# Expert loop of a two-block network: passes of 32 tokens in four bands instead of 64 in two, with the output product one pass behind

## The chip, the cores and the metric

The kernel runs as one program on one core of one Trainium2 chip. The metric is the device time in microseconds (us); lower is better. Engines are called PE (matrix products; PEld is its weight loads), DVE (vector engine), ACT (scalar engine), POOL (GpSimd) and SP (the engine whose queue issues the transfers here).

## What is computed

The reference takes 256 tokens of width 1024 through two blocks. The first holds attention, a gated recurrence and a table lookup with experts of one row each; the second holds a convolution, attention and a mixture of 32 experts. Only the last part, the mixture, is touched by the change. Cut down, it is:

```
logits = hf @ w_router + b_router            # 256 tokens, 32 experts
top_v, top_e = lax.top_k(logits, 4)
gates = softmax(top_v)
for each expert e, with the tokens xi that chose it:
    hc = xi @ w1[e] + b1[e]                  # 1024 -> 2048
    g, u = hc[:, :1024], hc[:, 1024:]
    g = minimum(g, 7.0); u = clip(u, -7.0, 7.0)
    hm = (u + 1.0) * (g * sigmoid(1.702 * g))
    y[token] += gate * (hm @ w2[e] + b2[e])  # 1024 -> 1024
x = x + g2 * y, then an RMS norm
```

All arrays are float32. An expert's weights are six units of 2 MB: four of `w1` and two of `w2`. All 32 experts have tokens, so 192 units (403 MB) are read whatever the routing is. Evaluating the reference's router on its own inputs gives the tokens of each expert, in order of the experts: 22, 36, 72, 24, 52, 13, 14, 43, 36, 29, 24, 24, 22, 39, 24, 18, 28, 58, 33, 26, 21, 21, 27, 18, 55, 38, 16, 28, 48, 44, 21, 50 (1024 in all). Experts count from 0 here.

## The kernel before

The arrays of an expert are read with a loop over passes. A pass is up to `NS` = 64 tokens of one expert; an expert with more tokens has more passes. The number of passes is known only at run time (`n_pass`, `passes_to`, `last_of`, `total_i`), and every engine runs its own loop over passes `q` and reads its tables with value loads.

On PE (`one_pass`, L1272) a pass is: `hidden` twice (L1240), the products of the 64 gathered tokens `xg` with `w1`, first the gate half into bank "Zg", then the up half into "Zu"; each product has 64 columns of stationary tokens and 512 moving weight columns, and the two halves of the 128 output partitions are two bands, `half`, that hold different weight columns. ACT copies each result to `z_sb`, `turn` (L1251) transposes it back, four 128x128 pieces each. Between these, `gather` (L1045) makes the next pass's tokens as products of `h3_rows` with the selection matrix `sel`, in two lots of eight, which ACT scales and shifts into `xg` (`modulated`, L1535). Then `combine(q)` (L1260) adds the rows `yg` of the pass before into the output in banks 0 to 3, the gated selection `selg` is transposed ("S", L1287), and the output product "D" (L1294 to L1298) multiplies this pass's `hm` with `w2`.

DVE makes `sel` for the next pass, adds the bias to the two transposed results (L2339), clips, multiplies, makes `hm` (L2349), then `selg` (L2096), then scales D's result into `yg` (L2357). The helper `mm` is L823, the helper `add` L982, transposes are L1256, L1287 and L1288.

The order of transfers is written out in SP's program. There are ten places of 2 MB: two sets of four for `w1`, of even and odd experts, and one pair (places 4 and 5) for `w2`. Ahead of the loop all six units of expert 0 and the four `w1` units of expert 1 are loaded. Then, for each expert e: after "Zg" of its last pass, the first two `w1` units of e+2; after "D" of its last pass, `w2` of e+1 and the other two `w1` units of e+2 (L717 to L727). All go through one queue.

## Time and profile before

| | |
|---|---|
| median of 3 runs | 2271.8 us (2269.18 to 2272.0) |
| the profiled execution, its own time | 2270.6 us |
| span in its profile | 2268.7 us |
| PE busy | 2073.9 us (91%) |
| DVE busy | 982.8 us (43%) |
| ACT busy | 599.0 us (26%) |
| mean granted clock of TensorE | 0.969 of 2.4 GHz |
| bytes moved | 784.36 MB |

The expert loop is the stretch from 1313 us to about 2261 us of the span. Busy time of PE is that of pipelined products whose ends are modelled, so a busy PE may be waiting inside. A float32 product stands in the trace as two MATMUL and two LDWEIGHTS records, a transpose as one of each. "PEclk" is the granted clock as a share of 2.4 GHz, so 0.50 is the level of 1.2 GHz and 1.00 that of 2.4 GHz. "DMA" is the busy share of the 16 transfer engines.

### The profile page before, as it was taken

Reading aid. Unit: us, or ns where it says so; the run is one execution under the profiler, and the core shown is the slowest. Engines: PE = TensorE matmul, PEld = TensorE weight load, DVE = VectorE, ACT = ScalarE, POOL = GpSimd, SP = SyncE. Lnnn points to the kernel's source line nnn. Section 1 sums busy time; section 2 is a strip of 40 time slices with the busy share of each in tenths; the row PEclk is TensorE's granted clock in tenths of the full one; section 3 lists DMA queues with packets and bytes.
Section 4 is the critical chain, followed back from the end, with each engine's and each line's share of the span. In section 5 each row is a group of like instructions: output and inputs, shape, how many; then the busy total and the mean of one; then the engine's idle time right before and its main releaser. Section 6 shows DMA issues by size and latency. Waiting matters only on the chain.

```text
span 2268.7 us, 27663 instructions
## 1 busy us (share of the span) xinstructions
PE 2073.9 (91%) x9026; PEld 1158.3 (51%) x9027; DVE 982.8 (43%) x2266; ACT 599.0 (26%) x1223; POOL 503.5 (22%) x562
## 2 busy tenths in 40 slices
PE   8999999988787778688999999999999999999998
PEld 7867788733333333233878744444444444433443
DVE  5955555756766766754573212111111111111112
ACT  4625401311212212222234122222222222222222
POOL 0000001677777777775000000000000000000000
PEclk9999999989889999999999999999999999999999
DMA  7352396899999999999644657899999999999996
GB/s 316 117 217 98 125 379 257 331 412 410 411 409 403 408 410 410 410 393 359 240 149 149 256 217 305 374 430 430 430 429 430 430 430 430 430 429 430 430 430 281
DMA packets 111704, 784.36 MB, mean 346 GB/s; under 512 B 13056, under 2 KB 13312, under 8 KB 80160
## 3 DMA queue, kind: packets, MB, share of 16 engines
q1 hardware_dynamic: 37920, 515.18, 54.7%
q0 software_dynamic: 73728, 268.47, 29.9%
q8 instruction: 31, 0.51, 0.1%
q14 instruction: 25, 0.20, 0.0%
HBM read 782.55 MB, written 1.05 MB: 345 GB/s over the span
## 4 chain that ended last, share of the span: by engine, by line
PE 49%; DMA 28%; POOL 11%; issue 6%; DVE 4%; ACT 2%; SPq 0%; DVEq 0%; POOLq 0%; ACTq 0%
PE ps L823 39%; DMA ring<-in_w_exp 23%; PE ps L982 8%; DMA ring<-in_peer_v,arena 4%; POOL ring L781 4%; POOL ring L783 4%; POOL arena L783 2%; POOL arena L781 1%; ACT arena L1333 1%; PE ps L1256 1%; DVE ring L2006 0%; SPq L692 0%; DVE arena L1955 0%; ACT arena L1427 0%; PE ps L955 0%
## 5 line engine op out<-in xcount | busy, mean ns | idle before, releaser
L823 PE MATMUL ps<-ring,arena 128*64 128x512 f32 (+2 forms) x2312 | 526.2, 586 | 32.9 <-DMA ring<-in_w_exp 30.2
L823 PE MATMUL ps<-arena,ring 128*128 128x256 f32 (+1 forms) x2272 | 488.1, 374 | 3.8 <-DVE arena L1749 3.2
L982 PE MATMUL ps<-ring,arena 128*128 128x512 f32 x768 | 386.1, 660 | 103.3 <-ACT arena L1333 103.2
L823 PEld LDWEIGHTS ps<-arena,ring 128*128 128x128 f32 x2272 | 419.3, 190 | 65.3 <-issue 7.8
L823 PE MATMUL ps<-arena 128*128 128x64 f32 (+4 forms) x2498 | 432.1, 419 | 11.6 <-ACT arena L1317 6.1
L823 PEld LDWEIGHTS ps<-ring,arena 128*64 128x64 f32 (+1 forms) x2312 | 177.0, 141 | 356.6 <-issue 300.4
L823 PEld LDWEIGHTS ps<-arena 128*128 128x128 f32 (+2 forms) x2498 | 266.8, 172 | 170.5 <-issue 160.5
L982 PEld LDWEIGHTS ps<-ring,arena 128*128 128x128 f32 x768 | 159.1, 212 | 325.7 <-issue 192.0
L2006 DVE CUSTOM_DVE_ANT_0 ring<-ring,ps 128x1024 f32<-128x1024 f32 x192 | 232.5, 1220 | 157.8 <-DMA ring<-in_peer_v,arena 156.9
L982 PE MATMUL ps<-arena 128*128 128x512 f32 (+2 forms) x600 | 201.9, 585 | 26.5 <-ACT arena L1333 24.8
L1661 ACT COPY arena<-ps 128x512 f32<-128x512 f32 (+1 forms) x99 | 51.0, 515 | 661.6 <-PE ps L823 628.9
L2339 DVE TENSOR_TENSOR arena<-ps,arena 128x512 f32<-128x512 f32 x66 | 45.7, 692 | 391.9 <-PE ps L1256 391.9
L781 POOL DMA_INDIRECT ring<-in_peer_u,arena x192 | 185.0, 963 | 80.0 <-issue 49.2
L783 POOL DMA_INDIRECT ring<-in_peer_v,arena x192 | 182.1, 948 | 59.8 <-issue 56.4
L982 PEld LDWEIGHTS ps<-arena 128*128 128x128 f32 (+1 forms) x600 | 83.3, 193 | 117.6 <-issue 80.8
L2357 DVE TENSOR_TENSOR arena<-ps,arena 128x512 f32<-128x512 f32 x33 | 22.8, 692 | 226.9 <-PE ps L823 226.9
L1324 ACT ACTIVATE arena<-arena 128x4 f32<-128x4 f32 (+1 forms) x67 | 19.9, 297 | 372.4 <-DVE arena L2006 372.4
L1333 ACT ACTIVATE arena<-arena 128x128 f32<-128x128 f32 x256 | 82.1, 390 | 121.7 <-DVE arena L2013 121.7
L1538 ACT ACTIVATE arena<-ps,arena 128x64 f32<-128x64 f32 x272 | 87.3, 400 | 26.8 <-PE ps L823 26.8
L2006 DVE CUSTOM_DVE_ANT_0 arena<-arena,ps 128x1024 f32<-128x1024 f32 x64 | 76.9, 1220 | 36.3 <-DMA arena<-in_peer_v,arena 35.9
L769 POOL COPY arena<-arena 128x16 uint32<-128x16 uint32 x16 | 3.3, 207 | 382.5 <-POOLq L768 382.4
L783 POOL DMA_INDIRECT arena<-in_peer_v,arena x64 | 60.6, 946 | 19.5 <-issue 17.7
(344 smaller groups left out, 1268.4 us busy)
## 6 DMA issues: line engine op xcount, KB each, us to landing
ring<-in_w_exp SPq DMA_DIRECT2D x128, 2048.0 KB, 24.9
arena<-in_w_exp SPq DMA_DIRECT2D x64, 2048.0 KB, 32.4
ring<-in_w_in SPq DMA_DIRECT2D x24, 2048.0 KB, 9.7
ring<-in_w_ada SPq DMA_DIRECT2D x12, 2048.0 KB, 8.6
ring<-in_w_out SPq DMA_DIRECT2D x4, 2048.0 KB, 8.3
ring<-in_w_peer_q SPq DMA_DIRECT2D x4, 2048.0 KB, 10.6
ring<-in_w_br_rnn SPq DMA_DIRECT2D x4, 1280.0 KB, 7.4
ring<-in_w_br_attn SPq DMA_DIRECT2D x2, 2048.0 KB, 14.1
```

The costliest lines, as they stand in the source:

```text
L781: pool.indirect_dma_start(out=uv_rows[k][:, 0:D], out_offset=None, in_=a["peer_u"], in_offset=at_k).then_inc(uv_full[k], 16)
L783: pool.indirect_dma_start(out=uv_rows[k][:, D:2 * D], out_offset=None, in_=a["peer_v"], in_offset=at_k).then_inc(uv_full[k], 16)
L823: return pe.matmul(o, l, r, start=start, stop=stop)
L982: return pe.matmul(o, l, r, start=start, stop=False, skip_group_check=True)
L1256: last = pe.transpose(ps[:, EXPERT_BANK[job], j * P:(j + 1) * P], z_sb[:, n, j * P:(j + 1) * P], ident)
L1324: fn(dots[:, par, some], dots[:, par, some], ACT.Gelu_apprx_tanh, scale=rcol[:, 4 * tile:4 * tile + 1]).then_inc(s_act, 1)
L1333: last = fn(diag[par][:, k, :], ident, ACT.Copy, scale=wts[:, par, k:k + 1])
L1538: own.mark(fn(xg[:, c, 0:NS], bank[:, j * P:j * P + NS], ACT.Identity, scale=scale2[:, c:c + 1], bias=mod[:, 3 * KD + c:3 * KD + c + 1]))
L1661: own(act.copy(dst, src))
L2006: last = dve.tensor_tensor_reduce(uv_rows[k][:, 0:D], uv_rows[k][:, 0:D], h2_rows[tile], 1.0, 0.0, ALU.mult, ALU.add, dots[:, par, k:k + 1])
L2339: own(tt(dst.rearrange("p j (h s) -> p j h s", h=2), ps[:, bank, :].rearrange("p (j h s) -> p j h s", j=4, h=2), bias.unsqueeze(3).to_broa ...
L2357: own(tt(yg, ps[:, EXPERT_BANK["D"], :], g2_halves, ALU.mult))
```

## The change

`NS` becomes 32, and the 128 output partitions are four bands of 32. One call of `hidden` now makes gate and up half together: for each of the eight pieces of the contraction four products of 32 stationary columns and 512 moving ones, one for each `w1` unit, into one bank "Z". So Z, its copy and its transposes are one each where they were two. The next pass's tokens are gathered the other way round: `sel` is stationary (32 columns), `h3_rows` moves (256 columns), the result "GR" has tokens in its rows; ACT copies it to `rows_now`, and `turn_rows` transposes it in two pieces ("GT"). DVE then scales and shifts all of it in two operations (in place of ACT's eight of L1538) into `xg`.

The output product is one pass behind: in pass q, `output(q, ...)` multiplies the `hm` of pass q-1, with the `w2` of the expert of pass q-1, whose number PE reads from `expert_before` by a value load. After the loop one more output product and two `combine` steps follow. In the first pass `hm` and `selg` are zeros, and the experts' output bias, a product of its own ahead of the loop before (`b2`), is now what the first `combine` adds.

SP's order is: after "Z" of the last pass of e, all four `w1` units of e+2 (`input_units`); `w2` of e after the "D" that follows the last pass of e-1, which is the "D" in the first pass of e (`output_units`). The places are the same: one pair for `w2`.

The diff, cut to its core:

```diff
-EXPERT_JOBS = (("Zg", 4), ("Zu", 5), ("Tg", 6), ("G0", 7), ("Tu", 4), ("G1", 5), ("S", 6), ("D", 7))
+EXPERT_JOBS = (("Z", 4), ("GR", 6), ("T", 5), ("S", 4), ("GT", 7), ("D", 5))
-NS = 64
+NS = 32
+GROUPS = P // NS
...
-            with sp.Fori(0, E // 2 - 1) as p:
-                for odd, places in ((0, (0, 1, 2, 3)), (1, (6, 7, 8, 9))):
-                    e = p * 2 + odd
-                    used(e, "Zg")
-                    load(e + 2, 0, places[0])
-                    load(e + 2, 1, places[1])
-                    used(e, "D")
-                    load(e + 1, 4, 4)
-                    load(e + 1, 5, 5)
-                    load(e + 2, 2, places[2])
-                    load(e + 2, 3, places[3])
...
+            def input_units(e, places):
+                X.filled(sp, last_pass(e), "Z")
+                for n in range(4):
+                    load(e + 2, n, places[n])
+
+            def output_units(e):
+                X.filled(sp, last_pass(e - 1) + 1, "D")
+                load(e, 4, 4)
+                load(e, 5, 5)
+
+            input_units(0, (0, 1, 2, 3))
+            with sp.Fori(0, E // 2 - 2) as p:
+                for odd, places in ((1, (6, 7, 8, 9)), (0, (0, 1, 2, 3))):
+                    e = p * 2 + (2 - odd)
+                    output_units(e)
+                    input_units(e, places)
...
+            def hidden(q, loaded, odd):
+                for n in range(4):
+                    pe.wait_ge(w_full[6 * odd + n], loaded)
+                X.claim(pe, q, "Z")
                 for c in range(KD):
+                    for n in range(GROUPS):
+                        last = mm(ps[n * NS:(n + 1) * NS, EXPERT_BANK["Z"], :], xg[:, c % 2, c // 2, :],
+                                  w1_unit[odd][n][:, c, :], c == 0, c == KD - 1)
...
+            def output(q, loaded, job):
+                pe.wait_ge(s_hm, q + 1)
+                for n in range(2):
+                    pe.wait_ge(w_full[4 + n], loaded)
                 X.claim(pe, q, job)
                 for j in range(4):
+                    for half in range(2):
+                        for n in range(2):
+                            g = (2 * half + n) * NS
+                            last = mm(ps[g:g + NS, EXPERT_BANK[job], :], hm[:, j, n * NS:(n + 1) * NS],
+                                      w2_unit[n][:, j, half * 512:(half + 1) * 512], j == 0, j == 3)
...
             def one_pass(q, pair, odd):
+                pe.wait_ge(s_xg, q + 1)
+                hidden(q, pair * 16 + 16, odd)
                 pe.wait_ge(s_sel, q + 2)
+                X.claim(pe, q, "GR")
+                filled_by(gather(EXPERT_BANK["GR"]), "GR")
+                pe.wait_ge(s_zc, q + 1)
+                X.claim(pe, q, "T")
+                for j in range(4):
+                    last = pe.transpose(ps[:, EXPERT_BANK["T"], j * P:(j + 1) * P], z_sb[:, j * P:(j + 1) * P], ident)
+                filled_by(last, "T")
                 combine(q)
+                turn_gates(q, "S")
+                pe.wait_ge(s_rows, q + 2)
+                X.claim(pe, q, "GT")
+                filled_by(turn_rows(EXPERT_BANK["GT"]), "GT")
+                before_q = pe.value_load(expert_before[0:1, bass.ds(q, 1)].bitcast(I32), min_val=0, max_val=E - 1)
+                output(q, before_q * 16 + 16, "D")
...
-                tokens(0, "G0")
-                tokens(1, "G1")
...
+                own(tt(xg, turned, by_chunk(scale2), ALU.mult))
+                dve.sem_inc(x_free[EXPERT_BANK["GT"] - 4], 1)
+                own(tt(xg, xg, by_chunk(mod[:, 3 * KD:4 * KD]), ALU.add))
+                dve.sem_inc(s_xg, 1)
```

On SP, the transfers of one expert in the loop before (L692 is the transfer, `expert_bank_full_4` is "Zg" and `expert_bank_full_7` is "D"; the value load is the table of last passes):

```order
L692 ISA [waits expert_bank_full_4]
L692 DMA ring<-in_w_exp 128x4096
L692 ISA
L692 DMA ring<-in_w_exp 128x4096
L714 TENSOR_LOAD arena
L714 ISA x2
L223 ISA
L692 ISA [waits expert_bank_full_7]
L692 DMA ring<-in_w_exp 128x4096
L692 ISA
L692 DMA ring<-in_w_exp 128x4096
```

and in the change (L699 is the transfer, `expert_bank_full_5` is "D", `expert_bank_full_4` is "Z"):

```order
L699 ISA [waits expert_bank_full_5]
L699 DMA ring<-in_w_exp 128x4096
L699 ISA
L699 DMA ring<-in_w_exp 128x4096
L721 ISA
L721 TENSOR_LOAD arena
L721 ISA x2
L227 ISA
L699 ISA [waits expert_bank_full_4]
L699 DMA arena<-in_w_exp 128x4096
```

The `w2` pair now waits by itself for a "D", and the four `w1` units follow in one lot after the "Z" wait that stands behind it.

On PE, the end of a pass before, from `combine` on (L982 is `combine`, L1287 and L1288 the transposes of `selg`, L823 the output product):

```order
L982 MATMUL ps<-arena 128x512 [waits gated_selection_transposed,expert_rows_ready]
L982 MATMUL ps<-arena 128x512 x3
L1287 MATMUL ps<-arena 128x128 [waits expert_bank_free_6,gated_selection_ready]
L1288 MATMUL ps<-arena 128x128
L1293 ISA [waits expert_hidden_ready,expert_bank_free_7]
L823 MATMUL ps<-ring,arena 64x512 [waits expert_unit_loaded_4]
L823 MATMUL ps<-ring,arena 64x512 x7
L823 MATMUL ps<-ring,arena 64x512 [waits expert_unit_loaded_5]
L823 MATMUL ps<-ring,arena 64x512 x7
```

and in the change (L1281 transposes `selg`, L1065 is `turn_rows`, L1313 the value load of `expert_before`, L832 the output product):

```order
L1281 MATMUL ps<-arena 128x128 [waits expert_bank_free_4]
L1281 MATMUL ps<-arena 128x128
L1065 MATMUL ps<-arena 128x128 [waits expert_bank_free_7,gathered_rows_copied]
L1065 MATMUL ps<-arena 128x128
L1313 ISA
L1313 TENSOR_LOAD arena
L1313 ISA x2
L1266 ISA [waits expert_hidden_ready]
L832 MATMUL ps<-ring,arena 32x512 [waits expert_bank_free_5,expert_unit_loaded_5,expert_unit_loaded_4]
L832 MATMUL ps<-ring,arena 32x512 x15
```

The output product has as many products (16) of half the stationary width; ahead of it stand two more transposes and a value load.

On DVE, behind the gated selection, before (L2357 makes `yg`) there is one operation:

```order
L2096 TENSOR_SCALAR arena<-arena 128x128
L299 REGISTER_ALU
L2357 TENSOR_TENSOR arena<-ps,arena 128x512 [waits vector_own,expert_bank_full_7]
L299 REGISTER_ALU
L2327 REGISTER_ALU [waits vector_own]
L2327 COMPARE_AND_BRANCH
```

and in the change (L2387 and L2389 scale and shift the gathered tokens, L2392 makes `yg`, L2396 `hm`):

```order
L2114 TENSOR_SCALAR arena<-arena 128x128
L303 REGISTER_ALU
L2387 TENSOR_TENSOR arena<-ps,arena 128x256 [waits vector_own,expert_bank_full_7]
L303 REGISTER_ALU
L2389 TENSOR_TENSOR arena<-arena 128x256 [waits vector_own]
L303 REGISTER_ALU
L2392 TENSOR_TENSOR arena<-ps,arena 128x512 [waits vector_own,expert_bank_full_5]
L303 REGISTER_ALU
L2396 TENSOR_TENSOR arena<-arena 128x256 [waits vector_own,expert_sigmoid_ready]
```

Two operations came in ahead of `yg`, and the multiplication that makes `hm` moved from ahead of `selg` to behind `yg`.

## Rows read from the trace of the kernel before

**Rows 1.** Busy time by stretch: us, busy us of each engine, PEclk, DMA share, GB/s

```profile
1310.00:1320.00 10.00, 9.39 (x38) 3.21 (x38) 0.48 (x2) 1.28 (x1) 0.00 (x0) 1.00 0.01 2
1320.00:1330.00 10.00, 10.00 (x61) 5.20 (x58) 1.20 (x3) 3.18 (x5) 0.00 (x0) 1.00 0.88 339
1330.00:1340.00 10.00, 10.00 (x55) 4.54 (x56) 3.20 (x7) 4.04 (x10) 0.00 (x0) 1.00 0.20 82
...
1390.00:1400.00 10.00, 10.00 (x48) 3.30 (x46) 1.44 (x5) 1.15 (x1) 0.00 (x0) 1.00 0.17 74
...
1410.00:1420.00 10.00, 10.00 (x67) 6.25 (x67) 4.40 (x9) 6.41 (x13) 0.00 (x0) 1.00 0.46 198
...
1430.00:1600.00 170.00, 170.00 (x900) 74.71 (x898) 33.46 (x72) 43.88 (x85) 0.00 (x0) 1.00 1.01 430
1600.00:2200.00 600.00, 571.28 (x3008) 249.64 (x3006) 115.92 (x249) 150.95 (x293) 0.00 (x0) 1.00 1.01 430
```

**Rows 2.** DMA issues, 1430 to 2230 us: count, KB each, median us to landing

```profile
ring<-in_w_exp SPq DMA_DIRECT2D x106, 2048.0 KB, 24.9
```

**Rows 3.** Timeline of PE, first pass: start us, us, engine, line, count of records

```profile
1310.67 1.88 PE L982 MATMUL ps<-arena 128*128 128x512 f32 x4
1313.16 13.96 PE L823 MATMUL ps<-ring,arena 128*64 128x512 f32 x64 [0.61 <-issue]
...
1327.54 1.90 PE L823 MATMUL ps<-arena 128*128 128x64 f32 x16
...
1331.55 1.99 PE L982 MATMUL ps<-arena 64*128 64x512 f32 x8
1333.46 0.33 PE L1287 MATMUL ps<-arena 128*128 128x128 f32 x1
1333.63 0.27 PE L1288 MATMUL ps<-arena 128*128 128x128 f32 x1
1333.83 7.09 PE L823 MATMUL ps<-ring,arena 128*64 128x512 f32 x32
1340.75 4.46 PE L823 MATMUL ps<-arena 128*64 128x512 f32 x20
```

**Rows 4.** The line that makes yg, all executions: ns min/median/max, first and last start

```profile
L2357 DVE TENSOR_TENSOR arena<-ps,arena x33: 691/692/693, 1341.0 to 2258.5; 128x512 f32<-128x512 f32 x33
```

**Rows 5.** The chain that ended last, from 2202 us on: start us, us, what

```profile
2202.31 24.87 DMA ring<-in_w_exp
2227.18 0.04 issue
2227.22 17.41 PE ps L823 x80
...
2251.41 7.04 PE ps L823 x32
...
2258.47 0.70 DVE arena L2357
...
2259.37 2.01 PE ps L982 x8
...
2264.47 0.75 DVE ring L2376
```

**Rows 6.** Groups of PE, 700 to 1300 us, full stationary width: count | busy us, mean ns

```profile
L823 PE MATMUL ps<-ring,arena 128*128 128x512 f32 x32 | 13.9, 592 | 0.0
```

**Rows 7.** PE's queue (PEldq): waits and control around the up half, value loads

```profile
L219 PEldq EVENT_SEMAPHORE  x1: 3647/3647/3647, 1706.1 to 1706.1; - x1
...
L219 PEldq EVENT_SEMAPHORE  x1: 51/51/51, 1713.0 to 1713.0; - x1
...
L1306 PEldq ALU_OP  x1: 32/32/32, 1700.1 to 1700.1; - x1
...
L1302 PEldq TENSOR_LOAD <-arena x1: 306/306/306, 1700.3 to 1700.3; - x1
...
L1304 PEldq TENSOR_LOAD <-arena x1: 299/299/299, 1701.1 to 1701.1; - x1
...
L1243 PEldq EVENT_SEMAPHORE  x1: 51/51/51, 1702.0 to 1702.0; - x1
```

**Rows 8.** Weight loads of PE, timeline at 1717 us

```profile
1717.74 1.86 PEld L823 LDWEIGHTS ps<-arena 128*128 128x128 f32 x16
```

**Rows 9.** Costliest groups of the page: ACT's scale and shift of gathered tokens

```profile
L1538 ACT ACTIVATE arena<-ps,arena 128x64 f32<-128x64 f32 x272 | 87.3, 400 | 26.8 <-PE ps L823 26.8
```

**Rows 10.** Timeline of DVE behind yg

```profile
1703.72 0.69 DVE L2357 TENSOR_TENSOR arena<-ps,arena 128x512 f32<-128x512 f32 x1 [7.49 <-PE ps L823]
1706.68 0.48 DVE L2099 TENSOR_SCALAR arena<-arena 128x128 f32 x2 [2.27 <-issue]
```

**Rows 11.** Timeline of SP: transfers issued

```profile
1320.44 22.63 SPq L692 DMA_DIRECT2D ring<-in_w_exp  x6
```

**Rows 12.** Timeline of PE around a long wait in the first block; then stretch by stretch

```profile
502.08 8.30 PE L982 MATMUL ps<-ring,arena 128*128 128x512 f32 x12 [3.71 <-ACT arena L1333]
...
502.00:510.30 8.30, 8.22 (x13) 3.56 (x14) 6.62 (x21) 1.24 (x6) 6.16 (x8) 0.64 1.03 410
```

More of the change, by code:

```diff
@@ L1043, in first_gates, with gather, turn_rows @@
                            c == KD - 1)
-            def gather(b, half):
-                for j in range(4):
-                    c = 4 * half + j
-                    for t in range(TT):
-                        last = mm(ps[:, b, j * P:j * P + NS], h3_rows[:, t, c * P:(c + 1) * P], sel[:, t, 0:NS],
+            def gather(b):
+                for t in range(TT):
+                    for n in range(GROUPS):
+                        last = mm(ps[n * NS:(n + 1) * NS, b, 0:QW], sel[:, t, :], h3_rows[:, t, n * QW:(n + 1) * QW],
                                   t == 0, t == TT - 1)
+                return last
+            def turn_rows(b):
+                for j in range(2):
+                    last = pe.transpose(ps[:, b, j * P:(j + 1) * P], rows_now[:, j * P:(j + 1) * P], ident)
                 return last
@@ L1196, in _ @@
                     for t in range(TT):
-                        last = pe.transpose(ps[0:E, b, t * P:(t + 1) * P], gate_rows[:, t, :], ident)
+                        for half in range(2):
+                            last = mm(ps[64 * half:64 * half + E, b, t * P:(t + 1) * P], gate_rows[:, t, :], ident,
+                                      True, True)
                     last.then_inc(full[b], 1)
@@ L1307, in _ @@
                         one_pass(q, pair, odd)
-            combine(total).then_inc(s_fin, 1)
+            combine(total)
+            turn_gates(total, "Z")
+            output(total, 16 * E, "T")
+            combine(total + 1).then_inc(s_fin, 1)
         @block.scalar
@@ L1532, in _, with modulated @@
                 last.then_inc(s_x2r, 1)
-            def modulated(bank, half):
-                for j in range(4):
-                    c = 4 * half + j
-                    own.mark(fn(xg[:, c, 0:NS], bank[:, j * P:j * P + NS], ACT.Identity, scale=scale2[:, c:c + 1],
+            def modulated(bank):
+                for c in range(KD):
+                    at_c = (c % 2) * P + (c // 2) * NS
+                    own.mark(fn(xg[:, c % 2, c // 2, :], bank[:, at_c:at_c + NS], ACT.Identity, scale=scale2[:, c:c + 1],
                                 bias=mod[:, 3 * KD + c:3 * KD + c + 1]))
@@ L2317, in _ @@
                     dve.wait_ge(s_poolM, 1)
-                    own(dve.tensor_copy(gT[0:E, :], ps[0:E, b, 0:T]))
+                    for half in range(2):
+                        rows = slice(64 * half, 64 * half + E)
+                        own.mark(dve.tensor_copy(selgT[rows, :], ps[rows, b, 0:T]))
+                    own.settle()
                     dve.sem_inc(free[b], 1)
-                    dve.sem_inc(s_gT, 1)
-            own(dve.tensor_copy(bias_now, b1[:, 0, :]))
-            select(selg, 0, 0, True)
+                    dve.sem_inc(s_selgT, 1)
@@ L2330, in _ @@
[L2330 to L2345 removed]
+                own.enter(q, 2 + 4 + 2 + 1 + 2 + 1 + 1)
@@ L2359, in _ @@
                 dve.sem_inc(s_yg, 1)
+                dve.wait_ge(s_sg, q + 1)
+                own(tt(hm, u, sg_act, ALU.mult))
+                dve.sem_inc(s_hm, 1)
                 own.leave_open()
             end = Own(dve, s_vend)
+            X.filled(dve, total, "T")
+            end(tt(yg, ps[:, EXPERT_BANK["T"], :], g2_halves, ALU.mult))
+            dve.sem_inc(s_yg, 1)
             dve.wait_ge(s_fin, 1)
```

243 lines of the change are left out of this document (112 added, 131 removed).

## The prediction

> **What bounds the kernel now.** I read the stretches first, then the timeline of one pass, then the chain that ended last. From 1430 to 2200 us the transfer engines are never idle: 1.01 busy at 430 GB/s [rows 1]. One unit is 2048 KB [rows 2], or 2.10 MB / 430 GB/s = 4.88 us, so the six units of an expert take 29.3 us. PE's pass takes 1340.7 - 1313.2 = 27.6 us [rows 3]. There are 33 passes [rows 4], which is what the token counts give at 64 a pass. So PE is the bound for the first passes and the transfers from then on; `yg` comes 33 times in 917 us. Where PE leads, the queue runs empty: its share is 0.20, 0.17 and 0.46 in three stretches of 10 us before 1430 [rows 1]. At the end the chain goes from a landing at 2227.2 through the last pass to 2268.7 [rows 5]. The bytes don't change. The change can gain only by emptying the queue less often or by a shorter end, and it loses wherever the queue empties anew.
>
> **The pass on PE after the change.** *Products.* A product of 512 columns with full stationary width is two records of 13.9 / 32 = 0.43 us [rows 6]; with two bands 64 records took 13.96 us, 0.22 each [rows 3], so two bands halve it exactly. I take it that four halve it again. Z is 32 products: 6.9 us (13.7 before). D is 16: 3.45 us (7.0 before [rows 3]).
>
> *Issue.* PE's queue must feed four instructions per product (two weight loads, two products). A wait of 3647 ns from 1706.1 ends at 1709.75, the 64 instructions of the up half follow, and the next control instruction is at 1713.0 [rows 7]: 50 ns each. Z needs 128 x 50 = 6.4 us, D 3.2, so the array still sets both, but narrowly, and the queue hardly gets ahead. Other rows give a worse end: 16 weight loads and their 16 products took 1.86 us, 58 ns each [rows 8], though full-width loads may be what is slow there. I take 50, since it comes from the same narrow loads.
>
> *Between Z and D.* Gather, 32 instructions, is issued by 1.3 us after Z's end; the transposes of z by 2.0; `combine` takes 1.9 (1.99 with its pipeline [rows 3]), to 3.9; four transposes 0.6. The value load (0.8 us from 1700.3 to 1701.1 [rows 7]) is issued beneath `combine`. D can start 4.6 us after Z. Bounds: 3.6 (array time alone) and 5.5 (58 ns each).
>
> *Between D and the next Z.* In the same expert 0.35 us, an estimate: the branch and some waits, about 0.1 us for each control instruction (two from 1700.1 to 1700.3 [rows 7]), less the 0.25 by which the issue of D ends first (3.45 - 3.2). With a new expert PE's queue does the branch and two value loads, 1700.1 to 1702.1 [rows 7]; before, these lay beneath 7 us of D already queued, now D's issue ends with D, so they show: 2.1 us. Bounds 0.5 and 2.1. A pass is 6.9 + 4.6 + 3.45 + 0.35 = 15.3 us, or 17.05 with a new expert.
>
> *Other engines.* ACT loses its eight operations of 400 ns a pass [rows 9]; DVE gets two of 256 columns before D ends, hidden by D's 3.45 us. DVE behind `yg` takes 2.27 us over two value loads [rows 10]; with four, at most 4.5, and with `yg` and `hm` 6.3 us after D. `sel` is wanted after 0.35 + 6.9 = 7.25: just hidden. If D got shorter than the two operations, `xg` would be late next.
>
> **The transfers.** Passes become 46: two each for experts 1, 4, 7, 8, 13, 17, 18, 24, 25, 28, 29, 31, three for expert 2. Queue order is w2(e), in(e+2), w2(e+1), in(e+3) ("in" the four `w1` units, 19.5 us; w2 9.8 us). There is one pair of places for w2, and it is free only after the first D of expert e. I carried the times over the 46 passes; idle time of the queue is the sum that counts.
>
> *Start.* The bias product (eight records, four shown at 1310.67 [rows 3]) and the wide gather leave the stretch ahead of the loop; I start Z at 1311 in place of 1313.2. It ends at 1317.9; issue 0.2 and 1.0 until data flow (issue at 1320.4 [rows 11], share 0.88 in 1320 to 1330 [rows 1]) give 1319.1. Through in(31) there are 178 units: 868.6 us, to 2187.7 were the queue never empty.
>
> *Experts 1 to 3.* in(2) ends at 1338.6, but w2(1) waits for the D in pass 1, 1311 + 17.05 + 14.95 = 1343.0, +1.2: idle 5.6. w2(2) likewise: 3.5. in(4) waits for the third Z of expert 2, which waits for a D that waits for w2(2): 13.2. w2(3): 5.6. Sum 27.9 us.
>
> *Each later expert with two passes.* Its first D frees w2's places early, but w2(e) stands behind in(e+1), so its second D waits some 13 us. From the last byte of w2(e): landing 1.3, D 3.45, new expert 2.1, Z 6.9, 4.6, D 3.45, next issue 1.2 = 23.0 us, while the queue holds only in(e+2), 19.5. Idle 3.5 us for each of ten (4 to 29): 35 us. Before, both D of an expert found their w2 landed, and nothing stood idle after 1430. Experts with one pass leave PE 12 us of slack and cost nothing.
>
> *The clock.* PE's 13 us waits matter twice. In the first block a wait of 3.71 us is followed by a granted clock of 0.64 over 8.3 us [rows 12], that is 6 us at 1.2 GHz and 3 us lost. The second D of experts 4, 7, 13, 17, 24 and 28 starts after such a wait, on the 23.0 us chain: 6 x 3.0 = 18 us. Bounds: 0 and 20.7 (six D at half clock throughout).
>
> *End.* w2(30) starts at 2187.7 + 27.9 + 35 = 2250.6 and lands at 2261.7; PE is there at 2262.8. D to 2266.2; w2(31) only then: 1.2 + 9.8 + 1.3, to 2278.5; D 3.45; `combine` and transposes 3.0; the extra D 3.45: 2288.4. From the end of the output product to the end took 2268.7 - 2258.5 = 10.2 [rows 5]: 2298.6, with the clock's 18 us 2316.6. From in(31)'s landing this end is about 50 us against 41, the one-behind product's own price.
>
> Before's execution took 2270.6 for a span of 2268.7, so 1.9 is added: **2318.5 us**. The median of before is 1.2 above that execution. The same rules with before's order and 27.6 us a pass give a span of 2271 for 2268.7, so I trust them to some 3 us.
>
> **The rivals.** *Shorter passes, queue never empty.* If PE's queue hides the value loads (0.5) and the middle is array time alone (3.6), the chain is 20.4 us: 0.9 idle per expert, 2261 us with a full clock, 2263 as time: faster. For it: before, the same loads cost nothing, beneath 7 us of D. Against: four bands leave no such cover, and the clock's rows [rows 12]. It decides only if the chain falls under about 21 us with the clock high; with the clock low it gives 2281. 9%.
>
> *Issue binds.* At 58 ns Z is 7.6, the middle 5.5, D 3.8; the chain is 25.3 and more is lost at start and end: 2361 + 2 = 2363. 15%. The Trainium skill (TensorE: Matmul & The Clock Gate, "Wait — 56ns, not 53.3ns?") puts the sequencer at about 62 ns per MATMUL; if it held for every instruction here, an estimate by that page is 2382. The 50 ns [rows 7] speak against it.
>
> *Bands don't overlap fully.* If two of the four overlap and no more, Z stays 13.7 and D 6.9: 2612 us. The exact halving [rows 3, 6] speaks against. 6% for anything above 2385. The Trainium skill (same page, "Measured speedup vs the span model") has three column bands at 2.38 times, not 3; by that efficiency an estimate with Z 8.6 and D 4.3 is 2380. The two bands of this trace show no such loss.
>
> *It isn't the change I read:* passes other than 46, or w2 not held back by D. 3%, either way.
>
> **How the numbers follow.** The forecast's case, 2300 to 2345, gets 61%, the stretch between it and the time before 6%. The range runs from 2278 (short middle, low clock) to 2380 (issue at its worst): outside lie the fast rival and the bands' failure, some 15%. A measurement tells about 0.2% (4.5 us) from no change. Slower by more: 61 + 15 + 6, 4 of the 6 between and 1 of the last 3: 87%; within it 2 + 2 = 4%; faster 9%.
>
> **What would show it.** The line for `yg` 46 times; Z in 6.9 us, D in 3.45; DMA share under 1 in dips after every expert with two passes, the long one near 1390; a wait of about 13 us on `in_w_exp` ahead of their second D; PEclk of 0.5 behind it; w2(31) issued after 2270. If the share stays 1.01 from 1430 on, or the second D never waits, the sum is wrong.

## The result and the profile after

| | before | after |
|---|---|---|
| median of the runs on one chip | 2270.5 us (2268.6 to 2272.0, 4 runs) | 2292.9 us (2290.1 to 2296.1, 4 runs) |
| ratio, with 95% interval | | 1.0100 (1.0082 to 1.0117) |
| profiled execution: own time, span | 2270.6, 2268.7 us | 2296.1, 2294.2 us |
| mean granted clock | 0.969 | 0.91 |

Slower by 22.4 us (19 to 27 by the interval). The prediction said slower, 2318.5 us in a range of 2278 to 2380: the sign and the range held, but the step forecast (some 47 us) was twice the one measured. The profiled execution is the longest of the four, 3.2 us above their median. Compared with it, span with span, the forecast is 2316.6 - 2294.2 = 22.4 us too high. That is what has to be found.

The page of the changed kernel, its costliest groups; the line for `yg` answers to [rows 4]:

```profile
L2392 DVE TENSOR_TENSOR arena<-ps,arena 128x512 f32<-128x512 f32 x46 | 31.8, 692 | 188.4 <-PE ps L832 188.4
```

46 passes, as counted. The timeline of PE over a whole pass of expert 2 (the first row is the output product of its first pass and Z of the second), which answers to [rows 3]:

```profile
1369.33 10.51 PE L832 MATMUL ps<-ring,arena 128*32 128x512 f32 x96
...
1385.74 10.51 PE L832 MATMUL ps<-ring,arena 128*32 128x512 f32 x96 [1.92 <-issue]
1396.04 1.07 PE L832 MATMUL ps<-arena 128*32 128x256 f32 x16
1397.06 0.66 PE L1306 MATMUL ps<-arena 128*128 128x128 f32 x4
1397.64 1.99 PE L991 MATMUL ps<-arena 64*128 64x512 f32 x8
1399.56 0.44 PE L1281 MATMUL ps<-arena 128*128 128x128 f32 x2
1399.84 0.38 PE L1065 MATMUL ps<-arena 128*128 128x128 f32 x2
1400.15 3.64 PE L832 MATMUL ps<-ring,arena 128*32 128x512 f32 x32
1403.61 1.91 PE L832 MATMUL ps<-arena 128*32 128x512 f32 x16
```

96 records are D and the next Z without a seam: 10.51 us for 48 products, so D is 3.5 and Z 6.9 (64 records that stood alone took 7.07 with the pipeline's end). Four bands halve the two-band time exactly, as taken. But from Z's end (1385.74 + 10.51 = 1396.25) to D's start at 1400.15 are 3.9 us, not 4.6. From one D to the next are 14.4 us. And the D that starts at 1400.15 stands in the last pass of expert 2: the Z at 1403.6 belongs to expert 3, and no gap stands between them, where the forecast has 2.1 us. The queue of PE says why. These are the loads of the next expert's first and last pass, and the branch ahead of them, in the same stretch:

```profile
L1322 PEldq ALU_OP  x1: 32/32/32, 1401.1 to 1401.1; - x1
L1318 PEldq TENSOR_LOAD <-arena x1: 299/299/299, 1401.3 to 1401.3; - x1
L1320 PEldq TENSOR_LOAD <-arena x1: 308/308/308, 1402.0 to 1402.0; - x1
L1320 PEldq SEQ_ASSERT  x1: 18/18/18, 1402.6 to 1402.6; - x1
```

The queue has given out all 64 instructions of D by 1401.1, 0.9 us after D began, and is through with both loads by 1402.6, a microsecond ahead of D's end. They take about as long as forecast, but lie beneath D.

The stretches, answering to [rows 1] (us, busy us of PE, PEld, DVE, ACT, POOL, PEclk, DMA share, GB/s):

```profile
1319.00:1430.00 111.00, 106.15 (x916) 39.74 (x912) 35.76 (x96) 32.37 (x46) 0.00 (x0) 0.98 0.83 340
1430.00:2200.00 770.00, 523.52 (x4285) 182.34 (x4288) 162.29 (x436) 143.84 (x200) 0.00 (x0) 0.84 0.98 414
2200.00:2255.00 55.00, 51.87 (x459) 19.10 (x448) 16.71 (x46) 15.64 (x23) 0.00 (x0) 1.00 0.92 379
2254.40:2255.40 1.00, 0.80 (x10) 0.52 (x12) 0.50 (x2) 0.37 (x1) 0.00 (x0) 1.00 0.01 0
```

Against 430 GB/s a stretch loses its length times (430 - rate) / 430: 23.2, 28.7 and 6.5 us. The last byte of w2(30) comes at 2254.4, and behind it the transfers pause, so 0.6 of the 6.5 lie past it: 57.8 us of idle queue up to that byte. The forecast had 27.9 + 35 + 18 = 80.9. From there to the end it had 38.2 (w2(30) begun at 2250.6 and 18 for the clock, plus 9.8, is 2278.4; the end 2316.6), and measured are 2294.2 - 2254.4 = 39.8. So the end is right within 1.6 us, and nearly the whole error lies in the queue's idle time.

The chain that ended last, from 2269 us on, which answers to [rows 5]:

```profile
2269.81 1.99 issue
2271.80 5.35 PE ps L832 x32
...
2277.17 0.70 DVE arena L2392
...
2278.07 1.99 PE ps L991 x8
2280.05 0.37 PE ps L1281 x2
2280.42 3.61 PE ps L832 x32
...
2284.86 2.01 PE ps L991 x8
```

It is the one forecast: D of the last pass waits for w2(31), then the extra D and the second `combine`. That D takes 5.35 us where the extra one takes 3.6; this is the 1.6 us. And a wait on w2 at an expert with two passes, here expert 4: timeline of PE, then stretches.

```profile
1460.62 6.41 PE L832 MATMUL ps<-ring,arena 128*32 128x512 f32 x32 [14.74 <-issue]
1466.84 7.93 PE L832 MATMUL ps<-arena 128*32 128x512 f32 x80
```

```profile
1449.00:1460.00 11.00, 0.00 (x0) 0.00 (x0) 0.00 (x0) 0.00 (x0) 0.00 (x0) 0.51 1.00 429
1460.00:1467.00 7.00, 6.38 (x36) 1.84 (x40) 0.00 (x0) 0.00 (x0) 0.00 (x0) 0.55 1.03 440
1467.00:1478.00 11.00, 11.00 (x104) 4.29 (x96) 3.39 (x9) 2.97 (x5) 0.00 (x0) 1.00 1.01 429
```

D takes 6.41 instead of 3.64 us, at the 1.2 GHz level: 2.8 lost, near the 3.0 of the sum.

The same trace prices this for all ten of the later experts with two passes. From one D to the next are 14.4 us at the full clock; what the interval behind the second D has above that is "slow D" below. The queue's idle time is read from a stretch of 24 us around the pause that follows. The stretches of experts 4 and 29:

```profile
1470.00:1494.00 24.00, 22.49 (x200) 8.22 (x188) 8.09 (x23) 8.15 (x12) 0.00 (x0) 1.00 0.84 342
2228.00:2252.00 24.00, 22.69 (x213) 7.89 (x209) 6.34 (x17) 4.90 (x7) 0.00 (x0) 1.00 0.97 400
```

| expert | PE's wait ahead of the second D, us | slow D, us | queue idle, us | idle less slow D |
|---|---|---|---|---|
| 4 | 14.7 | 2.8 | 4.9 | 2.1 |
| 7 | 11.8 | 2.7 | 4.5 | 1.8 |
| 8 | 1.9 | 0.0 | 1.6 | 1.6 |
| 13 | 12.2 | 2.3 | 4.2 | 1.9 |
| 17 | 11.3 | 1.5 | 3.1 | 1.7 |
| 18 | 2.0 | 1.7 | 3.3 | 1.7 |
| 24 | 11.1 | 1.6 | 3.2 | 1.6 |
| 25 | 2.2 | 1.7 | 3.6 | 1.9 |
| 28 | 11.6 | 2.8 | 4.2 | 1.4 |
| 29 | 1.8 | 0.2 | 1.7 | 1.5 |

The last column hardly moves: each expert empties the queue for some 1.7 us, and a slow D is added to that in full. Of the 34.4 us in all, 17.2 are the slow D (the 0.2 of expert 29 is that of the value loads, experiment 2) and 17.2 the rest. The sum had 18 and 35.

### The profile page after: what moved, and what is told of

Its sections match the earlier page's. It is cut to its first block, busy times and chain, and to the rows that moved or that the text cites. A ratio compares the mean times of both kernels' runs of the same rounds, so it can differ in the third digit from the quotient of the medians.

```text
span 2294.2 us, 31155 instructions
## 1 busy us (share of the span) xinstructions
PE 1877.0 (82%) x10122; PEld 1010.9 (44%) x10123; DVE 1023.2 (45%) x2476; ACT 558.6 (24%) x1037; POOL 496.9 (22%) x560
## 3 DMA queue, kind: packets, MB, share of 16 engines
HBM read 782.55 MB, written 1.05 MB: 342 GB/s over the span
## 4 chain that ended last, share of the span: by engine, by line
PE 54%; DMA 24%; POOL 7%; issue 6%; DVE 4%; ACT 2%; SPq 1%; DVEq 0%; POOLq 0%; ACTq 0%; PEldq 0%
PE ps L832 42%; DMA ring<-in_w_exp 10%; PE ps L991 10%; DMA arena<-in_w_exp 7%; DMA ring<-in_peer_v,arena 6%; POOL ring L793 3%; POOL ring L795 2%; POOL arena L795 1%; POOL arena L793 1%; DVE ring L2023 1%; SPq L699 1%; PE ps L1306 1%; ACT arena L1352 1%; PE ps L964 1%; PE ps L1281 0%
## 5 line engine op out<-in xcount | busy, mean ns | idle before, releaser
L832 PE MATMUL ps<-ring,arena 128*32 128x512 f32 (+2 forms) x3144 | 417.4, 632 | 175.7 <-issue 101.3
L832 PE MATMUL ps<-arena,ring 128*128 128x256 f32 (+1 forms) x2272 | 490.1, 376 | 3.8 <-DVE arena L1766 3.2
L991 PE MATMUL ps<-ring,arena 128*128 128x512 f32 x768 | 391.5, 668 | 100.8 <-ACT arena L1352 100.8
L832 PEld LDWEIGHTS ps<-arena,ring 128*128 128x128 f32 x2272 | 421.8, 191 | 64.9 <-issue 8.0
L832 PE MATMUL ps<-arena 128*32 128x512 f32 (+4 forms) x2618 | 299.7, 517 | 100.3 <-DMA arena<-in_w_exp 86.6
L832 PEld LDWEIGHTS ps<-ring,arena 128*32 128x32 f32 (+1 forms) x3144 | 130.4, 121 | 424.8 <-issue 423.5
L832 PEld LDWEIGHTS ps<-arena 128*32 128x32 f32 (+1 forms) x2618 | 143.6, 127 | 267.0 <-issue 246.8
L991 PE MATMUL ps<-arena 64*128 64x512 f32 (+2 forms) x704 | 225.0, 588 | 21.5 <-ACT arena L1352 18.9
L1684 ACT COPY arena<-ps 128x512 f32<-128x512 f32 x138 | 61.2, 443 | 736.2 <-PE ps L832 707.8
L2372 DVE TENSOR_TENSOR arena<-ps,arena 128x512 f32<-128x512 f32 x46 | 31.8, 692 | 325.8 <-PE ps L1306 325.8
L991 PEld LDWEIGHTS ps<-arena 64*128 64x128 f32 (+1 forms) x704 | 91.2, 192 | 123.2 <-issue 92.9
L2392 DVE TENSOR_TENSOR arena<-ps,arena 128x512 f32<-128x512 f32 x46 | 31.8, 692 | 188.4 <-PE ps L832 188.4
L2117 DVE TENSOR_SCALAR arena<-arena 128x32 f32 (+1 forms) x94 | 18.2, 239 | 167.0 <-issue 166.9
## 6 DMA issues: line engine op xcount, KB each, us to landing
ring<-in_w_exp SPq DMA_DIRECT2D x128, 2048.0 KB, 20.4
ring<-in_w_peer_q SPq DMA_DIRECT2D x4, 2048.0 KB, 10.7
```

The source lines that it names most:

```text
L832: return pe.matmul(o, l, r, start=start, stop=stop)
L991: return pe.matmul(o, l, r, start=start, stop=False, skip_group_check=True)
L1684: own(act.copy(dst, src))
L2372: own(tt(gu_act.rearrange("p j (m s) -> p (j m) s", s=NS), ps[:, bank, :].rearrange("p (m s) -> p m s", s=NS), bias_now.unsqueeze(2).to_br ...
L2392: own(tt(yg, ps[:, EXPERT_BANK["D"], :], g2_halves, ALU.mult))
```

## The experiments

In all of them the kernel before ran on the same chip, with medians of 2270.0 to 2272.0 us. My expectations call "recurrence" the rules of the prediction's sum as a small program: the end of every Z and D, the queue in its order, 4.88 us a unit. Before any experiment I had set it to the trace of after: 3.95 us between Z and D, and the value loads shown in 2.1 us except behind a slow D. That gave 2294. As the runs will say, its second setting was wrong.

**1. More or fewer passes.** Is the time set by the queue, or by PE's passes? Two kernels fix the number of passes of every expert. In the first, tokens beyond 32 of an expert are left out. The second has 2.0 in place of 1.0 below: tokens beyond 64 are left out, and experts with up to 32 make a second pass over nothing.

```
-                    own(ts(n_pass[:, 0, :], count, NS + 0.5, 1.0, ALU.is_gt, ALU.add))
-                    for limit in range(2 * NS, PARTS * NS, NS):
-                        own(stt(n_pass[:, 0, :], count, limit + 0.5, n_pass[:, 0, :], ALU.is_gt, ALU.add))
+                    own(ts(n_pass[:, 0, :], count, 1e6, 1.0, ALU.is_gt, ALU.add))
```

> Every expert gets exactly one pass: tokens beyond 32 of an expert are left out (14 passes of the 46 gone), all else as after. Theory (weights arrive at 29.3 us an expert, a lone pass is no bound and leaves no idle time in the queue): the idle time left is about that of the first experts, and my recurrence gives 2236, range 2230 to 2243; that is below the kernel before, whose queue had its start gaps too. Rival (the added work is in every pass, clock losses included): every expert then waits for its weights at half clock, so the time stays near 2270 to 2280.

> Every expert gets exactly two passes (empty ones compute zeros): 64 instead of 46 passes. Theory: each expert costs the queue its 29.3 us and an idle time of about 3 us, chain of 2 passes with the half-clock output product: recurrence 2352, range 2335 to 2370. Rival (TensorE bound per pass): 18 passes of 14.4 us more, 2293 + 259 = 2552. Rival (idle time comes only from three- and two-pass neighbours, not from isolated doubles): about 2300.

Measured: 2238.0 us (2234.8 to 2239.6; ratio 0.9858, 0.9842 to 0.9875) and 2328.2 us (2327.5 to 2328.5; ratio 1.0252, 1.0235 to 1.0269). The stretches of the first, then of the second, and the second's PE at one expert:

```profile
1319.00:1430.00 111.00, 67.67 (x548) 22.29 (x544) 20.86 (x56) 17.25 (x24) 0.00 (x0) 0.82 0.99 421
1430.00:2200.00 770.00, 443.55 (x3408) 140.32 (x3397) 127.66 (x343) 114.84 (x161) 0.00 (x0) 0.79 1.00 427
```

```profile
1430.00:2200.00 770.00, 720.35 (x6292) 268.38 (x6288) 237.13 (x637) 211.30 (x294) 0.00 (x0) 0.99 0.96 402
```

```profile
1554.58 10.73 PE L832 MATMUL ps<-ring,arena 128*32 128x512 f32 x96 [2.04 <-issue]
...
1569.21 6.21 PE L832 MATMUL ps<-ring,arena 128*32 128x512 f32 x56
```

With one pass each the transfers never stop from 1430 to 2190 us (the 427 has in it the pause ahead of the last w2), and the clock's fall at every wait (0.79) costs nothing, since PE has slack. It is the second passes that empty the queue. With two each my number was 24 us too high and outside my range. PE sets the time there: 14.4 + 14.4 us and one wait of 2.0 in each pair, some 31 us an expert against 29.3 of transfers, at a clock of 0.99. The wait of 2.0 stands ahead of the *second* D of an expert (the D at 1554.58, then D and the next expert's Z in one piece of 96 records). So the 2 us that I had read in the trace of after as value loads were the wait for w2. The piece of 96 takes 10.73 us where D and Z inside one expert take 10.51: behind a D that had to wait, a change of expert shows 0.2 us. This sent me back to the loads.

**2. The value loads alone.** One kernel takes both loads away from the change of expert, one adds two.

```
             def one_pass(q, pair, odd, next_end):
...
+                pe.reg_mov(next_end, pe.value_load(passes_to[0:1, bass.ds(pair * 2 + odd + 2, 1)].bitcast(I32),
+                                                   min_val=0, max_val=MAX_PASSES))
...
-                    begin = pe.value_load(passes_to[0:1, bass.ds(pair * 2 + odd, 1)].bitcast(I32), min_val=0,
-                                          max_val=MAX_PASSES - 1)
-                    end = pe.value_load(passes_to[0:1, bass.ds(pair * 2 + odd + 1, 1)].bitcast(I32), min_val=1,
-                                        max_val=MAX_PASSES)
+                    begin = pe.snap(this_end, min_val=0, max_val=MAX_PASSES - 1)
+                    end = pe.snap(next_end, min_val=1, max_val=MAX_PASSES)
+                    pe.reg_mov(this_end, end)
```

```
+                    for _ in range(2):
+                        pe.value_load(passes_to[0:1, bass.ds(pair * 2 + odd, 1)].bitcast(I32), min_val=0,
+                                      max_val=MAX_PASSES - 1)
                     with pe.Fori(begin, end) as q:
```

> At a change of expert TensorE's queue loads nothing: the end of the expert's passes is kept in a register, and the next expert's is loaded inside each pass, ahead of the output product. Theory from the trace of after (the two loads run from 1401.05 to 1403.2, beneath the output product that ends at 1403.8; the queue is 2.7 us ahead, so the loads never show): no change, 2293 within 4. Theory on record in the prediction (the loads show in full, 2.1 us on the chain of each expert with two passes): with 0.17 instead of 2.15 us my recurrence falls from 2294 to 2280, time 2279 within 5.

> Two more value loads (unused) at each change of expert, 0.77 us each. Theory from the trace of after (cover of 0.6 us is left behind the loads): 0.9 to 1.5 us come to stand open at each change of expert; where that lies on the chain that frees the w2 places, at 10 to 14 experts, it costs 10 to 25 us: 2305 to 2318. Theory on record (all of it already shows, slope 1 throughout): 1.5 us more at each, recurrence 2330. Rival (TensorE is off the path at these places): 2293.

Measured: without loads 2294.2 us (2293.7 to 2294.9; ratio 1.0102, after's is 1.0100), no change. With two more, 2305.4 us (2300.0 to 2307.0; ratio 1.0153, 1.0138 to 1.0168). In its timeline of PE the change of expert now has a gap:

```profile
1402.04 3.64 PE L832 MATMUL ps<-ring,arena 128*32 128x512 f32 x32
1406.52 1.93 PE L832 MATMUL ps<-arena 128*32 128x512 f32 x16 [0.84 <-issue]
```

From D's start to Z's start are 4.5 us in place of 3.5, so 1.0 of the next 1.5 us of loads shows, and it costs 12.5 us. The loads that the kernel has cost next to nothing. What they do cost stands behind a D that had to wait, here that of expert 29, first in after, then without loads:

```profile
2224.52 10.72 PE L832 MATMUL ps<-ring,arena 128*32 128x512 f32 x96 [1.82 <-issue]
```

```profile
2223.97 10.51 PE L832 MATMUL ps<-ring,arena 128*32 128x512 f32 x96 [1.76 <-issue]
```

That is 0.2 us, worth some 2.5 us of the time by the price just found, less than the 6 us between the fastest and the slowest run of after. The step "now D's issue ends with D, so they show: 2.1 us" is refuted by experiment.

**3. A longer middle.** The gather of the next tokens is issued twice.

```
                 X.claim(pe, q, "GR")
+                gather(EXPERT_BANK["GR"])
                 filled_by(gather(EXPERT_BANK["GR"]), "GR")
```

> The 16 gather products between hidden product and output product are done twice (the same result, written twice), so each pass lengthens by about 0.9 us (the gather's 1.07 us of the trace, less what hid behind other waits) and nothing else moves. Theory: the chain that frees the w2 places is on the queue's path at 14 double experts or more: recurrence 2309, range 2303 to 2315, idle time of the queue 66 to 81 us. Rival (transfers bound, TensorE's work hidden): 2293 within 3. Rival (each pass on the path): 46 x 0.95 = +44, 2337.

Measured: 2304.3 us (2302.5 to 2304.5; ratio 1.0148, 1.0131 to 1.0165). The line of the gather in PE's timeline:

```profile
1397.10 1.94 PE L832 MATMUL ps<-arena 128*32 128x256 f32 x32
```

1.94 us for 1.05 to 1.07: 0.9 more a pass costs 11.4 us, not 46 x 0.9 = 41. That is a slope of 12.7 us for each microsecond between Z and D, near one for each expert with two passes, and the same as for the loads (12.5 for 1.0).

**4. D back in the pass of its own tokens.** 32 tokens to a pass and all else as in after, only without the pass of delay (`hm` is made before `selg`, the extra D at the end goes).

```
             def output_units(e):
-                X.filled(sp, last_pass(e - 1) + 1, "D")
+                X.filled(sp, last_pass(e - 1), "D")
...
-                before_q = pe.value_load(expert_before[0:1, bass.ds(q, 1)].bitcast(I32), min_val=0, max_val=E - 1)
-                output(q, before_q * 16 + 16, "D")
+                output(q, pair * 32 + 16 * odd + 16, "D")
...
-            combine(total)
-            turn_gates(total, "Z")
-            output(total, 16 * E, "T")
-            combine(total + 1).then_inc(s_fin, 1)
+            combine(total).then_inc(s_fin, 1)
```

> The output product is taken in the pass of its own tokens again (32 to a pass, four bands and all else as after): the w2 places come free one pass earlier, but the second hidden product of an expert with two passes now waits behind its first output product, hence for w2, and holds back the input units of the expert after the next. Theory (order and release in the queue decide): the queue stands idle some 16 us at each such expert, recurrence 2453, range 2430 to 2475. Rival (being one pass behind is what costs, so that undoing it gives the loss back): 2270 to 2285.

Measured: 2456.3 us (2454.2 to 2457.0; ratio 1.0816). The stretch:

```profile
1430.00:2200.00 770.00, 479.29 (x3820) 171.34 (x3812) 144.96 (x390) 129.37 (x180) 0.00 (x0) 0.81 0.87 368
```

Here the queue loses 770 x 62 / 430 = 111 us. So the delay by one pass is no cost in itself. It saves 163 us, given passes of 32. What remains against it is that w2's places come free late.

**5. The scale and shift back on the scalar engine,** in eight operations.

```
+                X.filled(act, q, "GT")
+                modulated(ps[:, EXPERT_BANK["GT"], :])
+                own.settle()
+                act.sem_inc(x_free[EXPERT_BANK["GT"] - 4], 1)
+                act.sem_inc(s_xg, 1)
...
-                own(tt(xg, turned, by_chunk(scale2), ALU.mult))
-                own(tt(xg, xg, by_chunk(mod[:, 3 * KD:4 * KD]), ALU.add))
```

> The scalar engine scales and shifts the gathered tokens again, in eight operations, the vector engine's two operations go; nothing else moves. From the trace of after: the turned tokens are there at 1400.3, the vector engine is done with them at 1402.3, the output product ends at 1403.8. Eight operations of 0.40 us behind a table load of 1.28 us give 1405 to 1405.5. Theory: the next hidden product then waits 1.2 to 1.7 us in every pass, which costs the same as 1 us more between the products (11 us) or somewhat more: 2303 to 2315. Rival (off the path either way): 2293 within 3.

Measured: 2290.4 us (2286.7 to 2293.0; ratio 1.0097, 1.0079 to 1.0115), the same as after; I was wrong. The row of ACT and the D and Z of PE beside it:

```profile
1397.20 2.26 ACT L1557 ACTIVATE arena<-ps,arena 128x32 f32<-128x32 f32 x8 [0.19 <-ACT arena L1684]
```

```profile
1396.75 3.64 PE L832 MATMUL ps<-ring,arena 128*32 128x512 f32 x32
1400.20 7.94 PE L832 MATMUL ps<-arena 128*32 128x512 f32 x80
```

Eight operations of 32 columns take 2.26 us, 0.28 each in a row. I had used 8 x 0.40, but the 400 ns [rows 9] are the length of one operation, and in a row they overlap: the same line has 87.3 us for 272, 0.32 each. (One of 32 columns is 388 ns long.) And I had put a table load ahead of them that comes only behind. They end at 1399.5, 0.7 us before D ends. This part of the change brings nothing and costs nothing.

**6. A cure for the late places.** Taking D unit by unit shortens the chain at two ends: the place of the first unit comes free after half of D, and D can start when the first unit has landed.

```
             def output(q, loaded, job):
...
+                X.claim(pe, q, job)
                 for n in range(2):
                     pe.wait_ge(w_full[4 + n], loaded)
-                X.claim(pe, q, job)
-                for j in range(4):
-                    for half in range(2):
-                        for n in range(2):
-                            g = (2 * half + n) * NS
+                    for j in range(4):
+                        for half in range(2):
+                            g = (2 * half + j % 2) * NS
                             last = mm(ps[g:g + NS, EXPERT_BANK[job], :], hm[:, j, n * NS:(n + 1) * NS],
-                                      w2_unit[n][:, j, half * 512:(half + 1) * 512], j == 0, j == 3)
+                                      w2_unit[n][:, j, half * 512:(half + 1) * 512], n == 0 and j < 2,
+                                      n == 1 and j > 1)
+                    if n == 0:
+                        last.then_inc(s_first, 1)
...
             def output_units(e):
-                X.filled(sp, last_pass(e - 1) + 1, "D")
+                done = last_pass(e - 1)
+                sp.wait_ge(s_first, done + 2)
                 load(e, 4, 4)
+                X.filled(sp, done + 1, "D")
                 load(e, 5, 5)
```

> The output product is taken unit by unit (first all 8 products of one 512-column unit of w2, then the 8 of the other; the four bands then hold chunk parity instead of unit), and SP issues the next expert's first w2 unit as soon as the first half is through, the second behind the whole. Theory (the DMA queue's idle time at each double expert is what the change costs: it waits for an output product that comes one pass late): each wait of the queue shortens by about 1.7 us at the experts where it stood idle, and TensorE waits for the first unit alone, so the last unit's arrival is followed by half a product. My recurrence of queue and passes gives idle time 38.8 instead of 65.7 us and a time of about 2267, range 2260 to 2276, so level with the kernel before. Rival (TensorE's own pass, the 46 passes of 14.4 to 16.4 us, sets the time): no change, 2293 within 3. Second rival (what the queue loses per wait is SP's wake and the DMA's start, not the product): between, about 2285.

Measured: 2260.4 us (2257.2 to 2265.7; ratio 0.9954, 0.9940 to 0.9969): 33 us under after, and faster than the kernel before. The stretches, and PE at expert 4:

```profile
1319.00:1430.00 111.00, 109.84 (x972) 39.28 (x968) 37.24 (x100) 34.51 (x48) 0.00 (x0) 1.00 0.86 355
1430.00:2200.00 770.00, 556.75 (x4520) 184.33 (x4516) 170.50 (x457) 151.00 (x210) 0.00 (x0) 0.86 1.00 427
```

```profile
1452.27 3.64 PE L835 MATMUL ps<-ring,arena 128*32 128x512 f32 x16 [10.16 <-DMA ring<-in_w_exp]
1457.17 3.37 PE L835 MATMUL ps<-ring,arena 128*32 128x512 f32 x16 [1.26 <-DMA ring<-in_w_exp]
1460.36 7.92 PE L835 MATMUL ps<-arena 128*32 128x512 f32 x80
```

The first half of D, slow as it is (3.64 us for 16 records, of which 32 take 3.64 at the full clock), now runs while the second unit is still under way. From 1430 to 2200 the queue loses 5.4 us instead of 28.7.

The halves apart: one kernel keeps PE's wait for both units ahead of D and only frees the first place early, the other has only PE's split wait and frees both places together. Their edits, against the kernel just shown:

```
                 for n in range(2):
                     pe.wait_ge(w_full[4 + n], loaded)
+                for n in range(2):
                     for j in range(4):
```

```
-                sp.wait_ge(s_first, done + 2)
+                X.filled(sp, done + 1, "D")
                 load(e, 4, 4)
-                X.filled(sp, done + 1, "D")
                 load(e, 5, 5)
...
-                    if n == 0:
-                        last.then_inc(s_first, 1)
```

> Half of the edit that takes the output product unit by unit: SP may load the first w2 unit once the first half of the product is through, but TensorE still waits for both units before the product begins. Recurrence for the whole edit 26 us below after, for this half 16 us: scaled to the 33 us measured, about 2272, range 2265 to 2280. Rival (what helps is TensorE's split wait alone): 2290.

> The other half: TensorE waits for the w2 units one by one, SP frees both places together after the whole product. Recurrence 16 us below after, scaled to what was measured about 2272, range 2265 to 2280. Rival (what helps is the early release alone): 2290.

Measured: 2273.9 us (2271.2 to 2276.9; ratio 1.0021, 1.0011 to 1.0030) and 2270.8 us (2267.8 to 2273.1; ratio 1.0004, 0.9994 to 1.0014). The row from 1430 to 2200 of each:

```profile
1430.00:2200.00 770.00, 540.18 (x4444) 186.43 (x4440) 167.38 (x450) 147.90 (x205) 0.00 (x0) 0.85 0.99 422
```

```profile
1430.00:2200.00 770.00, 553.77 (x4484) 183.56 (x4480) 169.18 (x455) 150.58 (x211) 0.00 (x0) 0.86 1.00 424
```

Either half brings 19 or 22 us, and both together 33, less than the sum. From 1430 to 2200 the queue loses 14.3 and 10.7 us in the two, so they save 14.4 and 18.0 of the 28.7: together more than there was. Both halves share the new order of D's products, which I didn't run alone; in the first of the two, from one D to the next are still 14.4 us (1323.16 to 1337.58), so the order by itself didn't shorten the pass. The last kernel has this edit and that without value loads.

> Both edits: output product unit by unit, each w2 unit's place freed by itself, and no value load at a change of expert. Theory from the trace (loads are hidden): as the first edit alone, 2260 within 4. Theory on record (loads show): 2249 by the recurrence less the 7 us by which it was too high for the first edit alone, so 2242 to 2249. Against the kernel before, either is faster.

Measured: 2261.1 us (2258.7 to 2266.5; ratio 0.9959, 0.9947 to 0.9970), as the split alone. The loads are hidden there too.

## Why the prediction was right in sign and twice too large

*Right, and shown.* 46 passes; Z 6.9 and D 3.5 with four bands; the queue idle at experts with two passes and not at those with one (experiment 1); w2's places as the cause (experiment 6). The end: 39.8 us measured, 38.2 forecast. The new operations of DVE hidden by D (experiment 5 shows that either engine would do).

*Failed: "Issue".* I took 50 ns for each instruction from the up half [rows 7] and concluded that the queue hardly gets ahead and that D's issue ends with D. The row can't bear that. Its 64 instructions went out in 3.25 us, while their 32 records take the array 7.0 us [rows 3]: the queue stood well ahead there, and the 3.25 us are only an upper bound on what issuing them costs. In the profile of after, the branch behind D stands 0.9 us behind D's start where D didn't wait (1400.15 and 1401.1, shown above), and the same where it did, at expert 29 with D at 2224.52:

```profile
L1322 PEldq ALU_OP  x1: 32/32/32, 2225.4 to 2225.4; - x1
```

By then some 8 of D's 32 records have run, at 3.5 us for all, and the queue has given out the rest: 2.5 us of cover for what stands behind D. Two terms rest on this step.

*"With a new expert ... they show: 2.1 us."* In its place: nothing where D hadn't waited, 0.2 us where it had, and on the chain it always had. The sum had it on the chain of all ten experts: 1.9 us too much in each.

*"Between Z and D", 4.6 us.* In its place 3.9 to 3.95: the middle runs at the array's pace, near the lower bound of 3.6. By the slope of experiment 3, 0.65 us less is 8 us of the error.

With both corrected the chain is 23.0 - 1.9 - 0.65 = 20.4 us, 0.9 idle against 19.5 of the queue. Measured are 1.7 (the table above). The rest is a term that I had too small. From the end of the D that frees w2's places (1369.33 + 3.5 = 1372.8) to the D that needs the new units (1385.74) go 12.9 us, where the sum had 1.2 + 9.8 + 1.3 = 12.3; with two passes each, too, PE waits 2.0 us instead of 1.3 for these units. That adds some 0.7 us for each of the ten.

*The clock's 18 us* measured 17.0, in part by luck. The six slow D named took 2.3 us too much on average and not 3.0, 13.6 in all; two more, at experts 18 and 25, were slow by 1.7 behind waits of 2.0 and 2.2 us that the sum didn't charge.

So the errors are: later experts, 53 forecast and 34.6 measured up to the last byte of w2(30), -18.4; the start, 27.9 and 23.2, -4.7; the moment of the start and the rounding of the rates, -0.9; the end, +1.6. Together -22.4. In the start the first and the last pause were 2.6 and 2.5 us for 5.6 each, by the same two terms; the other two were 3.5 and 13.4, as forecast, and 1.2 more went at the first transfers.

Two slips of the sum touch nothing in it: at 58 ns Z's 128 instructions are 7.4 us and D's 64 are 3.7, not 7.6 and 3.8, and from in(31)'s landing to the end its own times give 2298.6 - 2251.9 = 46.7 us, not "about 50".

*The rival "shorter passes, queue never empty"* had the mechanism that came true: loads hidden and a short middle. It said that with the clock low it gives 2281. The middle was 0.3 us longer than its 3.6, and the restart of the queue 0.6 longer, so the time came between it and the forecast. I had given the pair 9% because I trusted one row on the queue's pace.

*"Issue binds"* and *"bands don't overlap fully"* are refuted by 10.51 us for 96 records. The Trainium skill ("TensorE: Matmul & The Clock Gate", "Measured speedup vs the span model") has three column bands at 2.38 times, not 3; four bands of float32 here give the full factor against two. The same page's 62 ns for a MATMUL on the sequencer, given for hardware decode off ("Wait — 56ns, not 53.3ns?"), taken for every instruction as in the prediction's estimate, does not hold here: the 96 records and their 96 weight loads would need 11.9 us and ran in 10.51. Taken for MATMUL alone it would need 6.0, which these rows can't test.

*Left open.* No run took the clock's fall away: that would need work for PE in just those waits, and was not tried. That a slow D costs its excess in full rests on the ten experts of one trace. More places for w2 were not tried either.

## What to carry to other kernels

A pace read where the queue stands ahead of its engine is a bound, not a price: look how far ahead it stands before charging what follows. With few buffers and one queue in fixed order, what counts is the chain from a landing to the next release. Write it out and compare it with what the queue still holds; here 1 us on it was worth some 13 us of 2290, and halving the piece that is waited for and freed was worth more than the whole change had lost. And a gap of the size that you expect is not yet the one you expect: the 2 us before a D looked like my value loads until a kernel with another pattern of passes put them in another place.

## What the runs showed of the hardware that I had not expected

- PE's queue is through with the 64 instructions of D when some 8 of their 32 records have run: 0.9 us behind D's start at the full clock, 1.7 us at the 1.2 GHz level (expert 4: D at 1460.62, the branch at 1462.3). So 3.5 us of products cover a branch and two value loads.
- A wait of only 2.12 us was followed by a stretch at the lower level. The timeline of PE in after, and stretches around it:

```profile
1353.23 8.34 PE L832 MATMUL ps<-ring,arena 128*32 128x512 f32 x60 [2.12 <-issue]
```

```profile
1353.50:1357.00 3.50, 3.50 (x20) 1.08 (x16) 0.00 (x0) 0.00 (x0) 0.00 (x0) 0.52 1.00 431
1357.00:1360.00 3.00, 3.00 (x32) 1.10 (x28) 1.12 (x2) 0.00 (x0) 0.00 (x0) 1.00 1.01 431
```

  The waits of 1.92 and 2.04 us quoted above were followed by full pace. With two passes each, 16 of 19 such waits between 1554 and 2133 us were, one of 2.20 us among them, and three were not, one of 1.99 us among them: the length of the wait alone doesn't tell.
- ACT's operation on 32 columns is 388 ns long and the one on 64 columns 400 [rows 9]; in a row they overlap, to 0.28 and 0.32 us each.
- Two units into an idle queue need 12.9 us from the product that frees their places to the product that uses them, for 9.8 us of transfer at the full rate.
